# A four-part layer stack on one core: the even layer's output projection in three rounded passes, six probability buffers instead of four, and the next ffn's first weights split after the fifth output tile

## The chip, the cores and the metric

The kernel runs on one core of one Trainium2 chip. The metric is the device time of one launch in microseconds (us), taken over several runs; beside it stands one profiled execution of the same program, from which all rows below come. TensorE is called PE in the rows, VectorE DVE, ScalarE ACT, GpSimd POOL and SyncE SP.

## The reference, cut to what matters

Two layers over 256 latent tokens and 256 context tokens of width 1024, float32 throughout. Each layer is half an ffn, a mixer, half an ffn, each with a residual and a layer norm:

```python
x = half_ffn(x, mod_l, 0, ffn_a, ...);  cx = half_ffn(cx, mod_c, 0, ffn_a, ...)
hl, hc = modulate(x, mod_l, 1), modulate(cx, mod_c, 1)
yc, yl = even_mixer(hc @ ev_w_in, hl @ ev_w_in, ...)      # layer 0; layer 1 has odd_mixer
x = layer_norm(alpha * x + gate(mod_l, 1) * (yl @ w_out), ln_g, ln_b)
x = half_ffn(x, mod_l, 2, ffn_b, ...)
# the same for cx in layer 0
```

The even mixer has two halves of 512 columns each. The first is attention with 8 heads of 64: context queries see the 256 context keys, latent queries see all 512 keys with a bias, and each row gets a softmax. The second is a two-way mLSTM with 4 heads of 128, whose output is centred and scaled per head. `yc` and `yl` are both halves side by side; `w_out` is 1024 x 1024.

## The kernel before

All activations lie feature-major: `h`, `m` and `y` (which is `m` under another name) are 8 tiles of 128 features by 512 tokens, context in columns 0 to 255, latent in 256 to 511. The stages follow each other: ffn0, even, ffn1, ffn2, odd, ffn3. Each engine's program is written out by hand in its own block, and semaphores order them; there is no planner. So what runs when is set by the order of the code in a block and by the `wait_ge` calls.

**Products in parts.** Nearly all products with the input and ffn weights are made in three passes: weights and inputs are each split into a rounded part (type fp32r, `w_hi`, `m_hi`), which ACT makes as a copy, and the rest (`w_lo`, `m_lo`), which DVE makes as a subtraction, in place. Then PE adds hi x hi, hi x lo and lo x hi. The output projection of the mixers (`out_proj`, lines 790, 800 and 807) does not do this: it multiplies float32 by float32 directly, and each such product of 128x512 shows in the trace as two MATMUL instructions (64 of L790 in the even stage for 32 calls).

**The attention stage** goes over 16 pairs of units (a unit is one head, one stream, one tile of 128 queries). In a round of four pairs, two are of context queries (256 keys) and two of latent queries (512 keys). For a pair p, PE makes the scores (L950), DVE the negated row maxima (`maxima`: L2480, or L2482 to L2484 with the bias, written to `probs`), ACT the exponentials (L1627), DVE the reciprocal and the scaling (L2492, L2495), PE four or eight transposes (L979), ACT copies them (L1638), PE weighs the values (`weigh`, L962) once in two pairs, and DVE copies the result to `y` (`attention_out`, L2580). On DVE `maxima(p + 1)` stands ahead of the scaling of pair p, and it begins with

```python
if p >= 2:
    dve.wait_ge(sem("na_pT_done"), 2 * p - 2)
```

because `probs` has four buffers: unit u writes buffer `u % 4`, which the transposes of the pair two earlier must have read.

**The mLSTM stage** follows, eight steps v of: DVE exponents (L2513), ACT exponentials (L1669, L1671), DVE products (L2556), PE (L1026), DVE quotients (L2522 and on). Behind each second one the head is centred, and ACT takes its squares (L1679).

**The output projection.** In the first half four output tiles d = 0 to 3 grow side by side, one input tile c after another. Between c = 2 and c = 3 PE transposes the mLSTM heads (`turn_heads`, L1035), and for d = 2 of c = 0 it waits until the last mLSTM banks are read. Tiles d = 4, 5 and 6 follow one by one, and tile 7 is made for the context stream and then the latent stream, with the sums for the layer norm (`norm_stats`, L772, L773, L778, L780) of the context inside the latter. DVE adds each tile to `h` (L2019, tile 7 L2040), ACT squares it (L1360), POOL keeps the running sums of both (L2716 and L2722). Behind tile 6 DVE makes the first two `w_lo` of the next ffn (`first_weights`, L1979) and folds the modulation (`fold`); ACT makes the `w_hi` (L1277) at the same place. `first_tile` of the ffn (L700, L701, L696) then begins with the first normalised tile. The odd stage ends in the same way, for the latent stream alone, with float32 products too.

## Time and profile before

| | |
|---|---|
| median of 3 runs | 1960.8 us (1959.03 to 1961.54) |
| the profiled execution's own time | 1961.69 us |
| its span, first to last instruction | 1960.0 us |
| mean granted TensorE clock | 0.967 of full speed |
| PE busy | 95% of the span |
| DVE, ACT, POOL busy | 69%, 35%, 15% |

A timeline row gives the start in us from the span's start, the duration in us, engine, line, operation, output<-input with shapes, and how many instructions were merged; in brackets stands the idle time of the engine ahead of it and what ended that. The end of a MATMUL is modelled, so the distance between starts says more than durations. The granted clock is given as a share of 2.4 GHz; its two levels are 1.2 and 2.4 GHz.

### The profile page before, as it was taken

The page shows a single profiled execution, that of the slowest core. Times are in us where ns is not written, and L with a number is a line of the kernel's source. Part 1 is how long each engine was busy: PE and PEld are TensorE (multiplying, and loading weights), DVE is VectorE, ACT ScalarE, POOL GpSimd, SP SyncE. Part 2 cuts the span into 40 slices and gives each one's busy share as a digit, 9 for nine tenths or more (in the row PEclk, how much of TensorE's full clock was granted, in tenths as well). Part 3 has the DMA queues.
Part 4 walks back from the last instruction along what each step waited for, and adds up shares of the span by engine and source line. Part 5 has one row for each costly group of instructions (what it writes and reads, how often), then busy time and mean ns, then how long its engine had stood idle before and what let it go on. Part 6 is the DMA issues. An engine that isn't in the chain of part 4 may idle for free. (4 is left out here: it accounts for less than half of the span.)

```text
span 1960.0 us, 25249 instructions
## 1 busy us (share of the span) xinstructions
PE 1862.0 (95%) x9616; PEld 1559.0 (80%) x9616; DVE 1354.9 (69%) x2331; ACT 692.2 (35%) x1143; POOL 301.9 (15%) x313
## 2 busy tenths in 40 slices
PE   6999999999997789899999999999999999989997
PEld 6888878898784455788887888888878898879997
DVE  7677777869975563877778357774687887564454
ACT  3222233345444431422224233222242543434443
POOL 0000001143000003400000232000044445140002
PEclk7999999999897899899999999999999999989999
DMA  9355444215431101454544233554234545405533
GB/s 360 129 195 204 171 188 166 98 56 138 151 147 59 44 1 43 165 201 171 207 152 174 102 123 122 211 193 153 107 111 169 214 175 204 170 3 186 198 150 111
DMA packets 43963, 290.17 MB, mean 148 GB/s; under 512 B 13916, under 2 KB 19676, under 8 KB 27232
## 3 DMA queue, kind: packets, MB, share of 16 engines
q1 hardware_dynamic: 35488, 271.13, 37.7%
q10 hardware_dynamic: 8384, 17.83, 2.4%
q8 instruction: 58, 0.95, 0.2%
q14 instruction: 33, 0.27, 0.0%
HBM read 272.16 MB, written 16.78 MB: 147 GB/s over the span
## 5 line engine op out<-in xcount | busy, mean ns | idle before, releaser
L1930 DVE CUSTOM_DVE_ANT_0 L<-slot 128x1024 f32<-128x1024 f32 x272 | 339.5, 1248 | 82.3 <-DMA slot<-in_ada_dram 75.1
L1277 ACT ACTIVATE w_hi<-slot 128x1024 fp32r<-128x1024 f32 x176 | 186.3, 1061 | 573.5 <-PE bank L681 558.2
L1979 DVE TENSOR_TENSOR w_lo<-slot,w_hi 128x1024 fp32r<-128x1024 f32 x176 | 216.8, 1234 | 204.4 <-ACT w_hi L1277 197.9
L676 PE MATMUL bank<-m_hi,w_hi 128*128 128x512 f32 (+1 forms) x1344 | 296.6, 363 | 3.2 <-ACT w_hi L1277 3.2
L681 PE MATMUL bank<-m_hi,w_lo 128*128 128x512 f32 (+1 forms) x1344 | 296.2, 363 | 0.1
L678 PE MATMUL bank<-m_lo,w_hi 128*128 128x512 f32 (+1 forms) x1344 | 296.1, 363 | 0.0
L676 PEld LDWEIGHTS bank<-m_hi,w_hi 128*128 128x128 f32 x1344 | 232.3, 189 | 43.1 <-ACT w_hi L1277 4.0
L681 PEld LDWEIGHTS bank<-m_hi,w_lo 128*128 128x128 f32 x1344 | 232.5, 189 | 39.7 <-DVE w_lo L1979 0.5
L678 PEld LDWEIGHTS bank<-m_lo,w_hi 128*128 128x128 f32 x1344 | 232.6, 189 | 39.3
L2160 DVE TENSOR_TENSOR down_lo<-slot,down_hi 128x1408 fp32r<-128x1408 f32 x64 | 108.8, 1716 | 116.1 <-ACT down_hi L1326 115.8
L739 PE MATMUL bank<-g_lo,down_hi 128*128 128x512 f32 (+1 forms) x770 | 154.7, 349 | 0.1
L739 PEld LDWEIGHTS bank<-g_lo,down_hi 128*128 128x128 f32 x770 | 126.7, 190 | 19.0 <-DVE g_lo L2166 0.6
L2714 POOL COPY L<-h 128x512 f32<-128x512 f32 (+1 forms) x6 | 3.7, 613 | 883.0 <-DVE h L2019 883.0
L1326 ACT ACTIVATE down_hi<-slot 128x1408 fp32r<-128x1408 f32 x64 | 87.5, 1377 | 146.6 <-PE bank L742 111.4
L733 PE MATMUL bank<-g_hi_mid,down_hi 128*128 128x512 f32 (+1 forms) x420 | 97.9, 361 | 1.9 <-ACT g_hi_mid L1336 1.6
L742 PE MATMUL bank<-g_hi_mid,down_lo 128*128 128x512 f32 (+1 forms) x420 | 88.7, 347 | 0.0
L733 PEld LDWEIGHTS bank<-g_hi_mid,down_hi 128*128 128x128 f32 x420 | 70.8, 191 | 19.9 <-ACT g_hi_mid L1336 10.1
L742 PEld LDWEIGHTS bank<-g_hi_mid,down_lo 128*128 128x128 f32 x420 | 69.5, 189 | 9.9
L2716 POOL TENSOR_TENSOR L<-L,h 128x512 f32<-128x512 f32 (+1 forms) x36 | 44.1, 1224 | 215.4 <-DVE h L2019 214.9
L1360 ACT ACTIVATE L<-h 128x512 f32<-128x512 f32 (+1 forms) x42 | 23.5, 560 | 139.6 <-DVE h L2019 134.9
L2733 POOL TENSOR_TENSOR h<-h,L 128x256 f32<-128x256 f32 x79 | 64.7, 851 | 38.7 <-DVE L L2048 38.7
L2019 DVE SCALAR_TENSOR_TENSOR h<-bank,mgate,h 128x256 f32<-128x256 f32 x70 | 30.8, 477 | 40.8 <-PE bank L800 26.9
(393 smaller groups left out, 2929.8 us busy)
## 6 DMA issues: line engine op xcount, KB each, us to landing
slot<-in_gateup_dram SPq DMA_DIRECT2D x44, 2048.0 KB, 8.1
slot<-in_ada_dram SPq DMA_DIRECT2D x34, 2048.0 KB, 8.1
slot<-in_down_dram SPq DMA_DIRECT2D x32, 1408.0 KB, 6.4
slot<-in_ev_in_dram SPq DMA_DIRECT2D x4, 2048.0 KB, 8.8
slot<-in_od_in_dram SPq DMA_DIRECT2D x4, 2048.0 KB, 9.5
R<-s_ops SPq DMA_DIRECT2D x16, 512.0 KB, 5.7
s_tables<-slot ACTq DMA_DIRECT2D x8, 768.0 KB, 3.3
R<-s_tables SPq DMA_DIRECT2D x8, 768.0 KB, 6.7
```

Of the source, the lines that this page charges most:

```text
L676: nc.tensor.matmul(bank[j][:, c0:T], w_hi[:, off, c, :], m_hi[:, c, c0:T], start=(c == 0), stop=False)
L678: nc.tensor.matmul(bank[j][:, c0:T], w_hi[:, off, c, :], m_lo[:, c, c0:T], start=False, stop=False)
L681: last = nc.tensor.matmul(bank[j][:, c0:T], w_lo[b][:, 2 * j + off, c, :], m_hi[:, c, c0:T], start=False, stop=(c == KT - 1))
L733: nc.tensor.matmul(out_d, down_hi[:, half, f % HALF, :], g_hi(f)[:, a:b], start=(f == 0), stop=False)
L739: nc.tensor.matmul(out_d, down_hi[:, half, f % HALF, :], g_lo[:, f, a:b], start=False, stop=False)
L742: last = nc.tensor.matmul(out_d, down_lo[k - 3][:, half, f % HALF, :], g_hi(f)[:, a:b], start=False, stop=(f == FT - 1))
L1277: nc.scalar.activation(w_hi[:, off, :, :].rearrange("p a b -> p (a b)"), slots[b][:, (2 * (f % 2) + off) * D:(2 * (f % 2) + off + 1) * D], ...
L1326: nc.scalar.activation(down_hi[:, half, :, :].rearrange("p a b -> p (a b)"), slots[k][:, half * HALF * P:(half + 1) * HALF * P], ACT.Copy) ...
L1930: ins = nc.vector.tensor_tensor_reduce(out=junk, in0=slots[k][:, t * D:(t + 1) * D], in1=csilu[s_], scale=1.0, scalar=0.0, op0=ALU.mult, o ...
L1979: nc.vector.tensor_tensor(w_lo[b][:, t, :, :].rearrange("p a b -> p (a b)"), slots[b][:, t * D:(t + 1) * D], w_hi[:, off, :, :].bitcast(F3 ...
L2160: nc.vector.tensor_tensor(down_lo[d % 2][:, half, :, :].rearrange("p a b -> p (a b)"), slots[3 + d % 2][:, half * HALF * P:(half + 1) * HA ...
L2733: nc.gpsimd.tensor_tensor(h[:, d, a:b], h[:, d, a:b], mean[:, a:b], ALU.subtract).then_inc(sem("c"), 1)
```

## The change

Three edits. (1) The even output projection becomes `even_out_proj`: inputs and weights are split like everywhere else, and PE makes three passes of fp32r products. ACT gets 8 rounded copies of `y` tiles and 8 of weight parts, DVE as many subtractions. Where they stand: `y` tiles 0 to 3 ahead of the mLSTM (ACT) and behind its first exponents (DVE); weight parts 0 to 2 on ACT behind the exponentials of v = 1, part 3 behind those of v = 6, parts 4 to 7 behind the squares of head 2; on DVE part 0 in v = 1, part 1 in v = 3, parts 2 and 3 in v = 7; `y` 4 to 7 and parts 4 to 7 behind the last `y` tile. (2) `probs` has six buffers, and `maxima(p)` waits for the transposes of the pair three earlier. (3) In the even and the odd stage `first_weights` and `fold` move from behind tile 6 to behind tile 4 on DVE, and on ACT from behind all squares to behind the fifth.

```diff
-        probs = [L[:, 0:T], L[:, T:2 * T], R[:, 12288:12288 + T], R[:, 5120:5120 + T]]
+        probs = [L[:, 0:T], L[:, T:2 * T], R[:, 12288:12288 + T], R[:, 5120:5120 + T], L[:, 6 * T:7 * T], L[:, 7 * T:8 * T]]
...
+            def even_out_proj(between):
...
+                def inputs_rest(c):
+
+                    lo("y", c)
+                    for d in range(4):
+                        last = nc.tensor.matmul(proj_out(name, d)[:, :], out_hi[d][:, c, :], m_lo[:, c, :], start=False, stop=(c == KT - 1))
+                        if c == KT - 1:
+                            last.then_inc(used[0] if d == 3 else sem("even_out_done"), 1)
+
+                take(0)
+                for c in range(KT):
+                    hi("y", c)
+                    for d in range(4):
+                        if c == 0 and d == 2:
+                            pe.wait_ge(sem("ml_out_read"), 2 * HEADS)
+                        if c == 0:
+                            hi("w", d)
+                            lo("w", d)
+                        nc.tensor.matmul(proj_out(name, d)[:, :], out_hi[d][:, c, :], even_y_hi[:, c, :], start=(c == 0), stop=False)
+                        nc.tensor.matmul(proj_out(name, d)[:, :], w_lo[0][:, d, c, :], even_y_hi[:, c, :], start=False, stop=False)
+                    if c:
+                        inputs_rest(c - 1)
+                    if c == 2:
+                        between()
+                inputs_rest(KT - 1)
+                take(1)
+                for d in range(4, KT - 1):
+                    pe.wait_ge(sem("r_ready"), before("r_ready", name) + d - 3)
+                    hi("w", d)
+                    for c in range(KT):
+                        nc.tensor.matmul(proj_out(name, d)[:, :], out_hi[d][:, c, :], even_y_hi[:, c, :], start=(c == 0), stop=False)
+                    for c in range(KT):
+                        nc.tensor.matmul(proj_out(name, d)[:, :], out_hi[d][:, c, :], m_lo[:, c, :], start=False, stop=False)
+                    lo("w", d)
+                    for c in range(KT):
+                        last = nc.tensor.matmul(proj_out(name, d)[:, :], w_lo[1][:, d % 4, c, :], even_y_hi[:, c, :], start=False, stop=(c == KT - 1))
...
+                    if name in ("even", "odd") and d == 4:
+                        for off in range(2):
+                            weights_hi(1 if name == "even" else 3, 0, off)
...
-                if name in ("even", "odd"):
-                    first_weights()
...
+                        if st == 0 and u >= 6:
+                            act.wait_ge(sem("na_pT_done"), u - 5)
...
+                    if hd == 0:
+                        act.wait_ge(full[0], 16 * (uses_before("ffn1")[0]))
+                        for d in range(3):
+                            out_weights_hi(d)
...
+                act.wait_ge(full[1], 16 * (uses_before("ffn1")[1]))
+                act.wait_ge(sem("ml_scores_done"), HEADS)
+                act.wait_ge(sem("ml_out_done"), 2 * HEADS - 1)
+                for d in range(4, KT):
+                    out_weights_hi(d)
...
-                first_weights(n)
-                fold(n + 1)
+                    if d == 4:
+                        first_weights(n)
+                        fold(n + 1)
...
-                    if p >= 2:
-                        dve.wait_ge(sem("na_pT_done"), 2 * p - 2)
+                    if p >= 3:
+                        dve.wait_ge(sem("na_pT_done"), 2 * p - 4)
...
+                        for d in {1: (0,), 3: (1,), 7: (2, 3)}.get(v, ()):
+                            out_weights_lo(d)
```

The order of PE's instructions from the last mLSTM product on, before the change (`m` holds `y`, `slot` the weights, L1035 the transposes of the heads; a row counts calls, each of which the float32 product turns into two instructions in the trace):

```order
L1026 MATMUL bank<-R 128x129 x20
L790 MATMUL bank<-m,slot 128x512 x12
L1035 MATMUL bank<-ident,R 128x128 x16
L790 MATMUL bank<-m,slot 128x512 x20
L800 MATMUL bank<-m,slot 128x512 x24
L807 MATMUL bank<-m,slot 128x256 x12
```

and the same place after it, for the end of the first half (the last four `inputs_rest` of c = 6 and c = 7 stand together) and the next tile:

```order
L839 MATMUL bank<-even_y_hi,out_hi 128x512
L840 MATMUL bank<-even_y_hi,w_lo 128x512
L826 MATMUL bank<-m_lo,out_hi 128x512 x8
L851 MATMUL bank<-even_y_hi,out_hi 128x512 x8
L853 MATMUL bank<-m_lo,out_hi 128x512 x8
L856 MATMUL bank<-even_y_hi,w_lo 128x512 x8
```

What was 8 calls for a tile is now 24, of a cheaper kind. DVE behind the last `y` tile, before (L2570 writes `y`, L1991 the gate, L2019 are the residuals of tiles 0 to 6, two each, then come the first weights and `fold`, and L2040 is tile 7):

```order
L2570 SCALAR_TENSOR_TENSOR m<-bank,ml_gn,R 128x512 x4
L1991 TENSOR_SCALAR mgate<-mods 128x16
L2019 SCALAR_TENSOR_TENSOR h<-bank,mgate,h 128x256 x14
L1979 TENSOR_TENSOR w_lo<-slot,w_hi 128x1024 x2
L2002 TENSOR_SCALAR mscale<-mods 128x16
```

and after (the same instructions have lines 2673, 2078, 2106, 2066 and 2089; L2127 is tile 7):

```order
L2673 SCALAR_TENSOR_TENSOR m<-bank,ml_gn,R 128x512 x4
L2639 TENSOR_TENSOR m_lo<-m,even_y_hi 128x512 x4
L2644 TENSOR_TENSOR w_lo<-slot,out_hi 128x1024 x4
L2078 TENSOR_SCALAR mgate<-mods 128x16
L2106 SCALAR_TENSOR_TENSOR h<-bank,mgate,h 128x256 x10
L2066 TENSOR_TENSOR w_lo<-slot,w_hi 128x1024 x2
L2089 TENSOR_SCALAR mscale<-mods 128x16
L2091 TENSOR_TENSOR mshift<-mscale,lnb 128x16
L2092 TENSOR_TENSOR mshift<-mshift,mods 128x16
L2093 TENSOR_TENSOR mscale<-mscale,lng 128x16
L2106 SCALAR_TENSOR_TENSOR h<-bank,mgate,h 128x256 x4
L2127 SCALAR_TENSOR_TENSOR h<-bank,mgate,h 128x256
```

Eight subtractions are new ahead of the first residual, and the first weights now stand ahead of the residuals of tiles 5 and 6. ACT in the mLSTM stage, from the exponentials of v = 1 to those of v = 2 (L1744 is what was L1671, L1742 what was L1669):

```order
L1744 ACTIVATE R<-bank,acol 128x128
L1719 ACTIVATE out_hi<-slot 128x1024 x3
L1742 ACTIVATE R<-R 128x4x128
L1744 ACTIVATE R<-bank,acol 128x384
L1744 ACTIVATE R<-bank,acol 128x256
```

The three copies L1719 are new there; the others kept their order.

## Rows read from the trace of the kernel before

**Rows 1.** The page: busy time of the engines.

```profile
PE 1862.0 (95%) x9616; PEld 1559.0 (80%) x9616; DVE 1354.9 (69%) x2331; ACT 692.2 (35%) x1143; POOL 301.9 (15%) x313
```

**Rows 2.** Timeline, even stage: three-pass tiles (L874 to L879), then 256-column products.

```profile
449.97 1.98 PE L874 MATMUL bank<-even_m_hi,part_hi 128*128 128x512 f32 x8
...
455.41 1.98 PE L874 MATMUL bank<-even_m_hi,part_hi 128*128 128x512 f32 x8
...
440.23 0.28 PE L851 MATMUL bank<-even_m_hi,first_hi 128*128 128x256 f32 x1
440.35 0.28 PE L852 MATMUL bank<-even_m_hi,w_lo 128*128 128x256 f32 x1
```

**Rows 3.** Timeline, the first half of the even output projection.

```profile
723.43 1.88 PE L790 MATMUL bank<-m,slot 128*128 128x512 f32 x4
...
725.55 8.85 PE L790 MATMUL bank<-m,slot 128*128 128x512 f32 x20 [0.24 <-DVE R L2533]
...
731.06 2.49 DVE L2567 TENSOR_TENSOR R<-R 128x512 f32<-128x512 f32 x4
...
750.84 3.39 DVE L2019 SCALAR_TENSOR_TENSOR h<-bank,mgate,h 128x256 f32<-128x256 f32 x8 [13.15 <-issue]
```

**Rows 4.** Timeline, from tile 4 to the first product of ffn1.

```profile
753.15 20.76 PE L800 MATMUL bank<-m,slot 128*128 128x512 f32 x48
...
773.75 5.34 PE L807 MATMUL bank<-m,slot 128*128 128x256 f32 x24
...
776.47 3.23 DVE L1979 TENSOR_TENSOR w_lo<-slot,w_hi 128x1024 fp32r<-128x1024 f32 x2 [1.64 <-ACT w_hi L1277]
...
780.73 0.70 PE L778 MATMUL bank<-h,mean_w 128*128 128x256 f32 x2 [0.77 <-DVE h L2040]
...
788.69 0.55 PE L700 MATMUL bank<-m_hi,w_hi 128*128 128x256 f32 x1 [1.59 <-ACT m_hi L1251]
```

**Rows 5.** The page: ACT and DVE weight parts, POOL's sums (mean ns last before the bar).

```profile
L1277 ACT ACTIVATE w_hi<-slot 128x1024 fp32r<-128x1024 f32 x176 | 186.3, 1061 | 573.5 <-PE bank L681 558.2
L1979 DVE TENSOR_TENSOR w_lo<-slot,w_hi 128x1024 fp32r<-128x1024 f32 x176 | 216.8, 1234 | 204.4 <-ACT w_hi L1277 197.9
...
L2716 POOL TENSOR_TENSOR L<-L,h 128x512 f32<-128x512 f32 (+1 forms) x36 | 44.1, 1224 | 215.4 <-DVE h L2019 214.9
```

**Rows 6.** Timeline, mLSTM stage: where ACT and DVE wait.

```profile
679.42 0.63 ACT L1669 ACTIVATE R<-R 128x512 f32<-128x512 f32 x1 [4.11 <-DVE R L2513]
...
681.51 0.23 DVE L2522 SCALAR_TENSOR_TENSOR R<-bank,R 128x2 f32<-128x2 f32 x2 [2.13 <-PE bank L1026]
...
723.63 0.23 DVE L2522 SCALAR_TENSOR_TENSOR R<-bank,R 128x2 f32<-128x2 f32 x2 [3.34 <-PE bank L1026]
```

**Rows 7.** Two rounds of attention by windows: us, busy and instructions by engine, clock, DMA.

```profile
610.41:626.29 15.88, 12.24 (x66) 6.63 (x68) 11.13 (x30) 8.67 (x24) 0.00 (x0) 0.82 0.00 0
626.29:641.17 14.88, 11.24 (x66) 6.25 (x68) 11.04 (x30) 8.67 (x24) 0.00 (x0) 0.84 0.00 0
```

**Rows 8.** Who DVE waited for, 593 to 662.8: total us, times, longest.

```profile
DVE col L2480 <- PE bank L979: 9.9, 6, 1.9
...
DVE L L2482 <- PE bank L979: 3.6, 4, 2.0
DVE R L2482 <- PE bank L979: 2.8, 4, 2.2
```

**Rows 9.** Timeline, the first round of attention.

```profile
600.66 0.47 ACT L1627 ACTIVATE R<-bank,col 128x256 f32<-128x256 f32 x1 [4.41 <-DMA s_local<-R]
...
604.89 0.42 DVE L2482 COPY R<-bank 128x256 f32<-128x256 f32 x1 [2.17 <-PE bank L979]
```

**Rows 10.** Timeline, the end of the odd stage.

```profile
1734.69 3.62 PE L807 MATMUL bank<-m,slot 128*128 128x256 f32 x16
...
1740.20 0.70 PE L778 MATMUL bank<-h,mean_w 128*128 128x256 f32 x2 [1.03 <-DVE h L2040]
```

**Rows 11.** Windows: PE's last mLSTM products (columns as in rows 7).

```profile
719.40:723.40 4.00, 4.00 (x20) 3.88 (x21) 0.89 (x4) 0.00 (x0) 0.00 (x0) 0.57 0.00 0
```

More of the change, by code:

```diff
@@ L793, in out_proj @@
                             last.then_inc(used[slot_pair[0]] if d == 3 else sem(f"{name}_out_done"), 1)
-                    if c == 2 and between:
-                        between()
                 take(slot_pair[1])
@@ L808, in out_proj @@
                                                 start=(c == 0), stop=(c == KT - 1))
-                        if c == 3 and s_ == 1 and name == "even":
+                    last.then_inc(used[slot_pair[1]] if s_ == 1 else sem("ctx_out_done"), 1)
+                norm_stats(name, 1)
+            def even_out_proj(between):
+                name = "even"
+                hi = lambda what, n: pe.wait_ge(sem("part_hi_ready"), EVEN_OUT_AT + OUT_HI.index((what, n)) + 1)
+                lo = lambda what, n: pe.wait_ge(sem("part_lo_ready"), EVEN_OUT_AT + OUT_LO.index((what, n)) + 1)
+                def inputs_rest(c):
[31 more added lines that the diff above has]
+                        last = nc.tensor.matmul(proj_out(name, d)[:, :], w_lo[1][:, d % 4, c, :], even_y_hi[:, c, :], start=False, stop=(c == KT - 1))
+                    last.then_inc(sem("even_out_done"), 1)
+                pe.wait_ge(sem("r_ready"), before("r_ready", name) + KT - 4)
+                hi("w", KT - 1)
+                lo("w", KT - 1)
+                for s_ in range(2):
+                    a, b = STREAMS[s_]
+                    for c in range(KT):
+                        nc.tensor.matmul(last_out(name, s_)[:, a:b], out_hi[KT - 1][:, c, :], even_y_hi[:, c, a:b], start=(c == 0), stop=False)
+                    for c in range(KT):
+                        nc.tensor.matmul(last_out(name, s_)[:, a:b], out_hi[KT - 1][:, c, :], m_lo[:, c, a:b], start=False, stop=False)
+                        last = nc.tensor.matmul(last_out(name, s_)[:, a:b], w_lo[1][:, 3, c, :], even_y_hi[:, c, a:b], start=False, stop=(c == KT - 1))
+                        if c == 3 and s_ == 1:
@@ L1036, in turn_heads @@
                         last.then_inc(sem("ml_turned"), 1)
-                out_proj("even", (0, 1), 0, turn_heads)
+                even_out_proj(turn_heads)
             def head_means(name, c0):
@@ L1648, in even, with out_inputs_hi, out_weights_hi @@
                     turned_probs(p)
+                def out_inputs_hi(c):
+                    act.wait_ge(*((sem("even_y0"), 2 * (c + 1)) if c < 4 else (sem("even_y1"), c - 3)))
+                    nc.scalar.activation(even_y_hi[:, c, :], y[:, c, :], ACT.Copy).then_inc(sem("part_hi_ready"), 1)
+                def out_weights_hi(d):
+                    nc.scalar.activation(out_hi[d][:, :, :].rearrange("p a b -> p (a b)"), slots[d // 4][:, (d % 4) * D:(d % 4 + 1) * D], ACT.Copy).then_inc(sem("part_hi_ready"), 1)
+                act.wait_ge(sem("na_probs_ready"), 2 * NA_PAIRS)
+                for c in range(4):
+                    out_inputs_hi(c)
                 slot_done[3] += 1
@@ L1692, in even @@
                 nc.scalar.activation(ml_var, ml_var, ACT.Sqrt).then_inc(sem("ml_var_ready"), 1)
+                for c in range(4, KT):
+                    out_inputs_hi(c)
                 squares("even", 0)
@@ L2571, in even @@
                                                    ALU.mult, ALU.mult).then_inc(sem("even_y1"), 1)
+                for c in range(4, KT):
+                    out_inputs_lo(c)
+                for d in range(4, KT):
+                    out_weights_lo(d)
                 out_residual(1, "even", (0, 1), 0)
```

51 lines of the change are left out of this document (34 added, 17 removed).

## The prediction

> **What bounds the kernel now.** I read the page first: PE is busy 95% of the span, DVE 69% [rows 1]. So a stage gets shorter either by fewer PE cycles or by taking away what PE waits for, and most stages offer little. Then I read three stretches in the timeline, those that the change touches: attention (593 to 663 us), the even projection with the norm behind it (723 to 789), and the end of the odd stage. The reader should see in each which engine the others wait for.
>
> In the even projection it is PE alone: 48 instructions of tiles 4 to 6 follow each other from 753.15 to 773.75, 6.87 us for a tile, while DVE had stood idle 13.15 us before the first residual [rows 3, 4]. In attention it is no single engine: in a round of four pairs PE, DVE and ACT are busy 12.2, 11.1 and 8.7 of 15.9 us [rows 7], and DVE waits for the transposes L979 16.3 us in all (9.9 + 3.6 + 2.8) [rows 8]. That is a chain: transposes of pair p - 1, maxima of p + 1, scaling of p, transposes of p.
>
> **Edit 1, three passes: the price of a product.** Tiles with the same operand types and shape run in the even stage already: 24 instructions take 455.41 - 449.97 = 5.44 us, 0.227 us each, at full clock [rows 2]. The tile costs 6.87 us now. So a tile of 512 columns gets 1.43 us cheaper. With 256 columns the distance is 0.12 us [rows 2], so a stream of tile 7 takes 24 x 0.12 = 2.9 us against 16 x 0.215 = 3.4 now (half of 0.429, which is 6.87 over 16). The Trainium skill ("TensorE: Matmul & The Clock Gate", Back-to-back issue gap) gives N / 2.4 GHz + 2.5 ns, 216 ns for 512 columns. By it a tile would take 5.18 us and the eight tiles another 2 us less, an estimate; the trace shows 227 ns where the weights change with each product, and I go by the trace.
>
> First half, walked through. PE starts at 723.43 and does four products (0.9 us), to 724.3. Then it waits for the bank that DVE frees, until 725.55 [rows 3]: a float32 pair of tiles filled that time until now, with 0.24 us left. The 28 products up to the head transposes take 6.35 us, to 731.9. The heads become ready from 731.06 on, the last at 733.55 (2.49 us for four [rows 3]); the transposes behind it end about 734.1. The other 64 products take 14.5 us, to 748.6. The last product of tile 0 is over 0.7 us earlier; its residual follows 0.26 us later and takes 0.85 (3.39 us for eight of L2019, two for a tile [rows 3]), and tile 4 needs its bank: start at 749.2 instead of 753.15 [rows 4]. **3.9 us.**
>
> Second half. Three tiles at 5.44 end at 765.5 instead of 773.75. The context stream takes 2.9 us, the latent stream has 16 instead of 8 products ahead of the norm's sums (1.9 us), and these need two float32 products of two instructions each, 0.9 us, before L778. That puts L778 at 771.3. Before it stood at 780.73, 0.77 us of this being the wait for DVE's L2040, which stood behind the first weights (3.23 us from 776.47) and `fold` [rows 4]. In the new order the context residual can be made at 768.7, when PE has it. **The stretch to L778 gains 9.4 us**, the 3.9 included. From L778 to the first product of ffn1, 788.69, a chain of DVE, ACT and POOL takes 7.96 us [rows 4]; nothing in it changes, so 9.4 us arrive at ffn1, which is bound by PE.
>
> **What hides the new work.** ACT: a weight copy costs 1.06 us [rows 5]. Three stand behind v = 1, where ACT has 4.11 us idle before 679.42 [rows 6]: 3.2 fit, 0.9 are left. Parts 3 to 7 lie in later idle stretches; without cover each would cost 1.06. Behind a late copy there stand the next exponentials, and PE and DVE wait for those. DVE: a weight rest costs 1.23 us [rows 5]. One stands in v = 1 where DVE waits 2.13 us, one in the like place of v = 3, two in v = 7 where it waits 3.34 for 2.5 [rows 6]. The four `y` rests and four weight rests behind the last `y` tile cost 4 x 0.65 + 4 x 1.23 = 7.5 us (0.65 from L2567, 2.49 us for four [rows 3]). The 13.15 us idle there [rows 3] shrink by about 3 us, since PE is earlier, and take it. The first residual queues behind them; I reckon about 743.5 for their end against 748.2 when it is due. So all of it is costed at nothing; from the other side, if each gap were short by a third, 2 to 3 us.
>
> The first weights behind tile 4 need the next ffn's slot 0, whose load is issued when the first half ends. If that is late, ACT's sixth square and DVE's sixth residual queue behind it. PE waits for neither, since tile 7 needs only the residual of tile 3; POOL does, with 1.22 us an addition [rows 5], two for a tile. By my walk it is through with tile 6 at 769.2, where the sums are wanted at 770.4. Slack is 1.2 us, so this edit costs nothing or, at worst, 1 us.
>
> **Edit 2, six buffers.** With the wait moved back by one pair, DVE no longer waits for L979. How much of the 16.3 us comes back elsewhere the trace doesn't show, so I bound it. From above: a round cannot be shorter than DVE's 11.1 busy us, and in the first round ACT is held by a DMA until 600.66 [rows 9] whatever DVE does; 16.3 less some 2 gives 14 us. From below nothing is excluded but a loss, as no wait is added that isn't met: say 3.5. In between I walk one round. `attention_out` behind a latent pair has only 0.8 + 0.2 + 0.9 us of DVE work ahead of it (two short maxima, reciprocal, scaling), where PE needs the eight transposes and the weighing, 3.3 to 4: a wait of 1.3 to 2. Another 0.5 us falls where maxima want scores that stand behind the weighing. So a round takes 11.1 + 1.8 to 2.5, about 13.3, against a mean of 15.4 [rows 7]: 2.1 us for each of two full rounds. In the first round the maxima at 604.89 [rows 9] move up to when their scores are there, about 602.9: 2.0. In the last round the tail of transposes, copies and weighing stays, and I take 1. **7 us**, nearer the lower bound than the upper since two engines besides DVE are busy over half the time.
>
> **Edit 3 in the odd stage.** PE ends tile 7 at 1738.3, makes the first two sums until 1739.2 and waits 1.03 us for L2040, to 1740.20 [rows 10]; this wait goes. The ffn3 weights have long been loaded. **1.0 us.**
>
> **Sum.** 9.4 + 7 + 1.0 = 17.4 us. The profiled execution took 1961.69 us, 1.7 more than its span, so it would take 1944.3. It lies 0.9 us over the median of 1960.8; from the median I get 1943.4, and forecast 1943.5.
>
> **The rivals.** Within 0.2% is 4 us, about what a measurement of this kernel can tell from no change.
>
> - *The forecast*, 1940 to 1947, chance 0.67.
> - *The attention waits come back*: PE, with weighing and scores in order and a clock of 0.82 [rows 7], or ACT takes DVE's place, and only 3 to 4 us are gained. 1947 to 1950, chance 0.13. For it speaks PE's 12.2 us in a round, against it that PE too waits for DVE before most transposes.
> - *Attention reaches DVE's bound*: 1936 to 1939.5, chance 0.07. A denser PE could also get a higher clock there.
> - *The side work shows*, or PE's 1.2 us wait at 724.3 brings the lower clock for some us. Just before it PE runs at 0.57 after a wait [rows 11], then at full clock in the projection. 2 to 5 us: 1945.5 to 1949, chance 0.07.
> - *Slower*, chance 0.03: the clock. PE needs 43.8 us for the new projection at 2.4 GHz (21.8 + 16.3 + 5.8). At 1.2 GHz all through it would need twice that and the kernel would take 1987; the sign turns when 17.4 of the 43.8 us are run at the lower level. The densest PE work has full clock in the trace, so it is unlikely. A second way to the same side are weight loads that are not hidden: 0.162 us each (1559.0 us for 9616 [rows 1]) on 24 products is 3.9 us a tile instead of nothing, which turns the gain of 1.43 into a loss of 2.4 and ends at 1974. Rows 2 show 24 loads inside 5.44 us, so I give it 0.01 of the 0.03. The Trainium skill ("TensorE: Matmul & The Clock Gate", What overlaps and what doesn't) has the rule behind it: a load overlaps with running products only where the row group differs, which full 128-row products never do. The trace does not agree.
> - *No change that can be told*: several of the gains fail together, chance 0.03.
>
> **How the numbers follow.** The likeliest case gives 1943.5. From 1938 to 1950 it takes in the forecast, the second and fourth case and part of the third, some 0.88 of the chance on paper; I keep that width because the size of edit 2 is bounded so loosely. Faster 0.94, same 0.03, slower 0.03.
>
> **What the changed profile would show.** Right: tile 4 of the projection starts 25.8 us after its first product instead of 29.7; tiles 4 to 6 are 5.4 us apart; no idle time of PE before the context L778; from the first product of the projection to the first of ffn1 55.8 us instead of 65.3; DVE waits for the transposes of L979 near zero, and instead for L962; rounds of 13 to 13.5 us; ACT's exponentials of v = 2 start no later behind those of v = 1. Wrong: rounds above 14.5 us, a DVE wait for ACT's weight copies, POOL ending its sums after PE wants them, or a granted clock below 1 between the first product and the norm.

## The result, and the profile after

The changed kernel takes 1939.43 us, median of 4 runs (1937.61 to 1942.06), the kernel before beside it 1960.72 (1959.03 to 1961.54). The ratio is 0.9889, 95% interval 0.9873 to 0.9906: 21 us faster, 4 us more than the 17.4 of my sum, and inside the range of 1938 to 1950. The profiled execution took 1940.38 us with a span of 1938.7, against 1961.69 and 1960.0.

The page of after, first part (beside [rows 1]):

```profile
PE 1848.0 (95%) x9688; PEld 1567.4 (81%) x9688; DVE 1368.4 (71%) x2347; ACT 704.7 (36%) x1159; POOL 302.5 (16%) x313
```

PE has 14 us less to do, although it has 72 instructions more; DVE and ACT got 13.5 and 12.5 us more, the parts of the projection's operands.

Timeline of after, the even projection (beside [rows 3] and [rows 4]): first product, the wait for the bank, the heads, the end of the first half, tiles 4 to 7, the context sums, ffn1.

```profile
717.21 0.47 PE L839 MATMUL bank<-even_y_hi,out_hi 128*128 128x512 f32 x1
...
719.40 0.50 PE L839 MATMUL bank<-even_y_hi,out_hi 128*128 128x512 f32 x1 [1.03 <-DVE R L2621]
...
725.89 2.17 PE L1094 MATMUL bank<-ident,R 128*128 128x128 f32 x16
...
742.02 3.23 DVE L2106 SCALAR_TENSOR_TENSOR h<-bank,mgate,h 128x256 f32<-128x256 f32 x8 [5.01 <-issue]
...
748.57 1.98 PE L851 MATMUL bank<-even_y_hi,out_hi 128*128 128x512 f32 x8
...
754.01 1.98 PE L851 MATMUL bank<-even_y_hi,out_hi 128*128 128x512 f32 x8
...
759.45 1.12 PE L864 MATMUL bank<-even_y_hi,out_hi 128*128 128x256 f32 x8
...
762.32 1.12 PE L864 MATMUL bank<-even_y_hi,out_hi 128*128 128x256 f32 x8
...
765.10 0.59 PE L784 MATMUL bank<-h,mean_w 128*128 128x256 f32 x2
...
772.95 0.55 PE L706 MATMUL bank<-m_hi,w_hi 128*128 128x256 f32 x1 [1.58 <-ACT m_hi L1310]
```

Tiles start 5.57 and then 5.44 us apart, a stream of tile 7 takes 2.87, the sums of L784 follow without idle time, and from the first product to ffn1 it is 55.74 us instead of 65.26. Tile 4 starts at 743.00, 25.79 us behind the first product.

Who DVE waited for in attention, after (592.5 to 655.5), beside [rows 8]:

```profile
DVE col L2568 <- PE bank L1009: 9.8, 4, 8.1
DVE m L2687 <- PE bank L1021: 8.7, 5, 4.0
DVE L L2570 <- PE bank L1009: 4.3, 4, 1.4
DVE R L2570 <- PE bank L1009: 1.2, 1, 1.2
```

The transposes (L1038 now, L979 before) are gone from the list; DVE waits for scores (L1009) and for the weighed group (L1021). The longest wait, 8.1 us, lies ahead of the stage's first maxima, as it did before.

**Stage by stage.** The same landmarks in several profiles, each stretch from one first instruction to the next (us; differences of starts in the timelines, the last column from the span rounded to 0.1 us). Between scan part and odd end lie 50.8 us that are alike in all of them:

```
                         attention  mLSTM  projection  ffn1,ffn2  odd: scan  odd: end  ffn3 to
                                           and norm    and on     part       and norm  the end
before                     68.96    60.50    65.26      788.52     106.69     12.28    213.03
before_again               68.91    60.50    65.26      788.61     106.73     12.29    212.87
after                      62.98    61.74    55.74      789.39     103.68     10.99    210.90
after_again                64.34    59.83    55.87      788.75     103.52     10.98    210.51
e1_attention               64.27    58.45    65.25      788.33     103.82     12.28    212.63
e2_projection              68.55    60.45    57.23      788.74     103.81     12.29    211.59
e3_first_parts             68.91    60.50    64.21      788.79     107.61     10.99    213.42
e4_late_first_parts        62.29    60.37    57.18      788.71     104.03     12.29    212.24
e5_scores_first            61.84    60.43    55.78      790.17     103.65     10.99    210.57
e6_bank_wait_filled        61.67    60.36    55.76      789.45     103.70     10.98    210.80
e7_act_waits               68.83    60.49    65.27      788.58     103.76     12.29    212.84
e8_pe_waits                70.95    59.98    65.30      788.85     103.65     12.29    211.33
e9_wait_kept               68.80    60.41    55.76      789.44     103.64     10.98    210.44
e10_scale_first            59.73    62.60    55.72      788.36     103.66     10.98    211.11
```

The two profiles of the comparison differ by 21.3 us: 1.5 ahead of attention (before_again reaches it at 591.53, before at 593.97, so this differs between executions of one program), 6.0 in attention, -1.2 in mLSTM, 9.5 in projection and norm, -0.9 in the ffns, 3.0 in the scan part, 1.3 at the odd end, 2.1 in ffn3. The stretches from attention to norm and the odd end give 15.6 (17.4 forecast, 1.8 less); scan part and ffn3, which no edit touches, give 5.1. That is what the experiments had to explain.

### The profile page after: what moved, and what is told of

The parts are those of the page before. It is cut to its first block and busy times, and to the rows that moved or that the text cites. A ratio compares the mean times of both kernels' runs of the same rounds, so it can differ in the third digit from the quotient of the medians.

```text
span 1938.7 us, 25445 instructions
## 1 busy us (share of the span) xinstructions
PE 1848.0 (95%) x9688; PEld 1567.4 (81%) x9688; DVE 1368.4 (71%) x2347; ACT 704.7 (36%) x1159; POOL 302.5 (16%) x313
## 5 line engine op out<-in xcount | busy, mean ns | idle before, releaser
L745 PEld LDWEIGHTS bank<-g_lo,down_hi 128*128 128x128 f32 x770 | 126.6, 190 | 19.1 <-DVE g_lo L2253 0.9
L706 PE MATMUL bank<-m_hi,w_hi 128*128 128x256 f32 x112 | 38.5, 358 | 19.7 <-ACT m_hi L1310 14.4
```

The source lines that it names most:

```text
L745: nc.tensor.matmul(out_d, down_hi[:, half, f % HALF, :], g_lo[:, f, a:b], start=False, stop=False)
```

## The experiments

Measured times are medians of 4 to 12 executions (before_again has one). In brackets stand the ratio to the kernel before on the same chip and its 95% interval. The ratio isn't always that of the two medians, and a gain "by the ratio" is reckoned from it. In the expectations, theory A and theory B are the two answers that the run should tell apart. They count the mLSTM stage between other landmarks than the table (56.5 us there are 60.5 here).

**Each edit alone, and the change without edit 3.** e1_attention is the kernel before with edit 2. These are its two main places; the buffers' indices and the `col` tile change with them, and ACT gets twelve waits:

```diff
-probs = [L[:, 0:T], L[:, T:2 * T], R[:, 12288:12288 + T], R[:, 5120:5120 + T]]
+probs = [L[:, 0:T], L[:, T:2 * T], R[:, 12288:12288 + T], R[:, 5120:5120 + T], L[:, 6 * T:7 * T], L[:, 7 * T:8 * T]]
-                    if p >= 2:
-                        dve.wait_ge(sem("na_pT_done"), 2 * p - 2)
+                    if p >= 3:
+                        dve.wait_ge(sem("na_pT_done"), 2 * p - 4)
```

> Only edit 2 (six probability buffers). Theory A, each edit gives in its own stretch what the profiles of before and after show there: attention gets 6.0 us shorter (68.96 to 62.98 us between the first scores and the first mLSTM product), the mLSTM stage keeps its 56.5 us since no projection work lies in it, and the kernel gains 6 us: 1954 to 1955.5. Theory B, the buffers also set something later in motion, so that the gain of some 4 us that my sum doesn't explain (odd stage and ffn3) comes with them: 1950 to 1952.

Measured 1951.22 us (0.9946, 0.9933 to 0.9960). e2_projection is the kernel before with `even_out_proj` and the parts it needs:

```diff
-                out_proj("even", (0, 1), 0, turn_heads)
+                even_out_proj(turn_heads)
```

> Only edit 1 (even projection in three passes). Theory A: 30 us of float32 tiles become 25.8 up to tile 4, tile 5 and 6 and the last tile follow as after the whole change, but the first weights of ffn1 still lie behind tile 6 on DVE, so PE's wait before the context sums comes back (0.8 us or more); mLSTM pays 1.4 us for the weight copies in it. Net 7 to 8 us: 1952.5 to 1954. Theory B, the unexplained 4 us belong to this edit: 1948 to 1950. Rival on the mLSTM stage: if its 1.4 us were only a matter of clock episodes and not of the added copies, this kernel's mLSTM stage lasts 56.5 us and not 57.8.

Measured 1948.21 us (0.9930, 0.9916 to 0.9943). e3_first_parts:

```diff
                     residual(n, name, d, proj_out(name, d), c0)
-                first_weights(n)
-                fold(n + 1)
+                    if d == 4:
+                        first_weights(n)
+                        fold(n + 1)
```

with the same move on ACT.

> Only edit 3 (the next ffn's first parts beside the fifth output tile, in the even and the odd stage). Theory A: PE's waits before the norm's sums go, 0.77 us in the even stage and 1.03 in the odd one: 1.8 to 2 us, 1958.8. Theory B, it also gives the 4 us in odd stage and ffn3: 1954 to 1956. Rival: DVE and GpSimd in each other's way behind tile 4 make the residuals late and give back some of it: 1960 to 1961.

Measured 1956.11 us (0.9973, 0.9963 to 0.9983). e4_late_first_parts is the whole change with this last diff undone.

> The whole change without edit 3 (the first parts stand behind tile 6 again, in both stages). Theory A: with the faster projection PE overtakes DVE more than before, since the tiles' residuals come every 5.44 us and the parts still take 3.2 us: the wait before the context sums is 0.8 to 2 us, the odd stage has its 1.03 us wait again, so this kernel is 2 to 3 us slower than the whole change: 1941.5 to 1942.5. Theory B, edit 3 is worth nothing by itself: within 0.5 us of the whole change.

Measured 1943.14 us (0.9904, 0.9889 to 0.9919), 3 to 4 us slower than the whole change (2.7 by the stretches of the table). The timeline of e4_late_first_parts shows the wait that comes back, and what DVE does at the time:

```profile
765.67 0.70 PE L784 MATMUL bank<-h,mean_w 128*128 128x256 f32 x2 [1.21 <-DVE h L2126]
...
761.37 3.26 DVE L2065 TENSOR_TENSOR w_lo<-slot,w_hi 128x1024 fp32r<-128x1024 f32 x2 [1.65 <-ACT w_hi L1336]
...
765.14 0.47 DVE L2126 SCALAR_TENSOR_TENSOR h<-bank,mgate,h 128x256 f32<-128x256 f32 x1
```

In its own stretch each edit gives about what theory A says: attention 4.7 us (6.0 expected), projection and norm 8.0, edit 3 1.05 in the even and 1.3 in the odd stage. Beside the faster projection edit 3 is worth 1.3 to 1.4 in the even stage, since PE overtakes DVE by more.

The weight copies cost nothing in the mLSTM stage. It lasts 60.45 us with them (e2_projection) and 60.50 without, but 58.45 in e1_attention, which has no copies either, and 61.74 in the first profile of after. Windows of the stage, before, e1_attention and after:

```profile
662.93:723.43 60.50, 51.46 (x224) 34.17 (x225) 38.99 (x140) 23.52 (x68) 0.00 (x0) 0.92 0.10 35
657.55:716.00 58.45, 49.40 (x224) 32.47 (x225) 38.99 (x140) 23.52 (x68) 0.00 (x0) 0.94 0.10 37
655.47:717.21 61.74, 52.70 (x225) 35.20 (x225) 45.85 (x148) 31.71 (x77) 0.00 (x0) 0.89 0.09 35
```

Stretch minus busy time is PE's idle time: 9.04, 9.05 and 9.04 us, and 9.0 to 9.1 in all 14 profiles. Only the busy time of the same products differs, and with it goes the granted clock, 0.94 to 0.88. So neither the copies nor any other edit makes PE wait more in this stage.

But the medians of the three kernels lie where theory B put them, or nearer to it than to theory A. Each edit alone gained more than its stretch: 10.6, 13.7 and 5.3 us by the ratios, 29.6 in all, where the three together give 22. The difference is less certain than it looks: each gain has an interval of 2 to 2.8 us to either side, and all three are measured against the same 13 executions of the kernel before, whose median of 1961.47 is the highest on record (1959.3 to 1960.8 in the other sets). In the profiles 2.9 us of the surplus of e1 and of e2 lie in the scan part of the odd stage, and 2.05 of e1's in mLSTM, by the clock. For e3 the profile doesn't show it: that execution took 1959.90 us, the longest of nine (from 1953.21).

**The same kernels again.**

> The changed kernel once more, for a second profile. Theory A, of the 21.3 us between the two profiles some 4 have no edit in their stretch (odd stage's scan part 3.0, ffn3's end 1.8, start of attention 1.5, against it mLSTM's loss): those that are luck of the clock or of a transfer differ again between this profile and the first. Theory B, they belong to the program: every stretch repeats within 0.3 us.

> The kernel before once more, for a second profile. Theory A, its odd stage shows a GpSimd wait of 1.8 us with half clock behind it only in some executions, so that this profile lasts 2 to 3 us less there. Theory B, the wait and the half clock are there again (scan part 106.7 us), and the changed kernels' 103.8 is something they gain by being earlier or later against the loads.

Measured 1939.50 us (0.9884, 0.9864 to 0.9903) and 1959.18 (one run). Theory A fell for the scan part: 106.73 us again in the kernel before, 103.52 in the changed one. It held for attention (64.34 against 62.98) and mLSTM (59.83 against 61.74), and the stretch ahead of attention (593.71 against 592.49).

**A change of nothing but instruction streams.** e7_act_waits is the kernel before with

```diff
                         src = score_banks[u % 4][:, 0:keys] if st == 0 else probs[u % 4][:, :]
+                        if st == 0 and u >= 6:
+                            act.wait_ge(sem("na_pT_done"), u - 5)
```

> The kernel before, with nothing but the twelve extra waits that the six buffers bring to ScalarE's instruction stream, each already fulfilled; no buffer, no operation and no order is changed. Scan part of the odd stage (first L1087 to first L1183): 106.7 us in both profiles of before and 107.6 with edit 3 alone, 103.7 to 103.9 in the six others, whatever edit they hold. Theory A, where the instruction fetches fall decides whether that stage's table lands late (an instruction fetch of ScalarE's and the small engines' queue stands 0.6 us before the landing in all three slow profiles and in none of the others): it takes 103.8 us here, kernel 1957 to 1958.5. Theory B, the 3 us come with an edit's own work or with being some 8 us earlier: 106.7 us, kernel as before, 1960.5. Attention 68.9 us by both.

and e8_pe_waits the kernel before with 302 such calls in front of the transposes, which make 151 instructions of PE (`EXTRA[u]` is 20 or 18 for even u, else 0):

```diff
+                        for _ in range(EXTRA[u]):
+                            pe.wait_ge(sem("even_acol_ready"), 2)
                         pe.wait_ge(sem("na_probs_ready"), u + 1)
```

> The kernel before, with 151 more instructions in PE's stream that only wait for what is long fulfilled, spread over attention where PE idles: as many as the three-pass projection adds. From the first product of ffn3 to the end: 212.9 to 213.4 us in the profiles without edit 1, 210.5 to 212.2 with it, by waits for copies of down weights whose transfers land late. Theory A, the shift of PE's instruction fetches decides it: 211 to 212 us here, and the kernel 1 to 2 us faster unless the waits cost as much in attention (bounds 0 to 3 us). Theory B, it doesn't: 213 us, the kernel as before or slower by what attention shows. Scan part of the odd stage stays at 106.7 us by both.

Both took the 3 us out of the scan part in their profiles, and e8 1.5 to 1.7 out of ffn3 too. First the kernel before, then e7_act_waits, both in the timeline, PE at the end of the scan part:

```profile
1666.88 2.21 PE L1117 MATMUL bank<-slot,R 128*128 128x64 f32 x16 [1.77 <-POOL slot L2800]
```

```profile
1663.44 1.97 PE L1117 MATMUL bank<-slot,R 128*128 128x64 f32 x16 [0.53 <-POOL slot L2802]
```

And windows of the two, ten us from the start of that product (columns as in [rows 7]):

```profile
1666.88:1676.88 10.00, 10.00 (x50) 7.24 (x51) 5.70 (x8) 7.36 (x17) 4.38 (x4) 0.83 0.01 2
```

```profile
1663.44:1673.44 10.00, 10.00 (x64) 8.09 (x65) 6.77 (x10) 8.80 (x18) 4.29 (x4) 1.00 0.01 2
```

The wait is 1.2 us shorter, and behind it PE's granted clock stays at 1.00, where behind the long wait it falls to a mean of 0.83: 1.2 us come of the wait and 1.7 of what follows it. The wait begins with a table (`s_tables`) whose transfer lands late: 10.7 us after its issue at 1634.24 in the kernel before, 9.5 in e7_act_waits, 8.2 in e8_pe_waits. The DMA answers from 2.2 us ahead of that issue on to the landing, before, e7_act_waits and e8_pe_waits:

```profile
q14 instruction: 1, 0.01, 0.6%
q8 instruction: 1, 0.02, 0.4%
slot<-in_od_in_dram SPq DMA_DIRECT2D x1, 2048.0 KB, 10.5
```

```profile
q8 instruction: 1, 0.02, 0.7%
slot<-in_od_in_dram SPq DMA_DIRECT2D x1, 2048.0 KB, 9.3
```

```profile
q14 instruction: 1, 0.01, 0.8%
slot<-in_od_in_dram SPq DMA_DIRECT2D x1, 2048.0 KB, 8.6
```

A transfer of instructions starts between the issue and the landing of this table in none of the 14 profiles. What differs is how many stand just ahead of it, beside the start of the 2048 KB weight load: one of queue 8, 2.0 to 2.5 us ahead of the table's issue, and one of queue 14, 1.1 to 1.6 us ahead. With both, in before, before_again and e3_first_parts, the table took 10.2 to 11.2 us to land; with that of queue 8 alone, in e7_act_waits and e1_attention, 9.5 and 9.2; with that of queue 14 alone, in e8_pe_waits, 8.2; with none, in the eight others, 8.3 to 8.9. So the recorded expectation of e7_act_waits has the time of the transfer wrong (0.6 us before the landing), and e8_pe_waits still has the transfer of queue 14 that theory A blamed, without a late landing. That the two transfers together hold the table up goes with all 14 profiles, but is argued and not shown.

In the executions that weren't profiled the effect can't be told from nothing. e7_act_waits took 1959.25 us; it gains 2.2 us by its ratio (0.9989, 0.9978 to 1.0000) and 0.4 by the two medians, and neither theory's kernel time (1957 to 1958.5, 1960.5) was met. e8_pe_waits gains nothing (0.9997, 0.9985 to 1.0009; 1959.36 us), having lost 2.0 us in attention by its own waits. So two kernels with nothing but fulfilled waits added have a scan part that is 3 us shorter in their profiles; how often the late landing meets an execution that isn't profiled is not known. That e8 changes the scan part too was expected by neither theory.

**What edit 2 consists of, and what bounds a round now.** e9_wait_kept is the changed kernel with

```diff
-                    if p >= 3:
-                        dve.wait_ge(sem("na_pT_done"), 2 * p - 4)
+                    if p >= 2:
+                        dve.wait_ge(sem("na_pT_done"), 2 * p - 2)
```

> The changed kernel with six buffers, but the wait of the maxima for the transposes left where it stood before (pair p - 2 instead of p - 3). Theory A, the gain of attention (4.6 to 7.3 us) is this wait alone: attention back at 68.5 to 69.5 us, DVE waiting some 16 us for the transposes again, kernel 1945 to 1946.5. Theory B, a part comes from elsewhere (another place in memory for two of the buffers, ScalarE's exponentials): attention 65 to 67 us.

Measured 1945.05 us (0.9920, 0.9906 to 0.9935). Who DVE waited for in its attention:

```profile
DVE col L2568 <- PE bank L1038: 9.6, 6, 1.8
...
DVE L L2570 <- PE bank L1038: 5.8, 6, 2.2
DVE R L2570 <- PE bank L1038: 0.7, 2, 0.5
```

16.1 us for the transposes, as the 16.3 of [rows 8], and 68.80 us for the stage. Theory A holds: the gain is this wait, 5 to 7 us.

What it is made of shows in windows of the whole stage, before, e9_wait_kept, after and after_again:

```profile
593.97:662.93 68.96, 49.82 (x258) 26.82 (x257) 44.52 (x120) 34.97 (x98) 0.85 (x3) 0.78 0.09 39
593.72:662.52 68.80, 49.72 (x259) 26.69 (x257) 44.55 (x120) 36.66 (x102) 0.85 (x3) 0.78 0.09 39
592.49:655.47 62.98, 47.70 (x258) 25.93 (x257) 44.22 (x120) 36.16 (x102) 0.85 (x3) 0.81 0.10 42
593.71:658.05 64.34, 49.33 (x259) 26.20 (x257) 44.26 (x120) 36.14 (x102) 0.85 (x3) 0.79 0.10 41
```

PE stands idle 19.1 us with the old wait and 14.9 to 15.3 with the new one, in all five profiles that have this attention (these two, e1_attention, e4_late_first_parts and e6_bank_wait_filled): 3.9 to 4.2 us are waits that went. The rest of the gain, 0.5 to 3.2 us, is PE's busy time, 49.8 us before and 49.4 to 46.6 after, and goes with the granted clock, 0.79 to 0.83 instead of 0.78.

e5_scores_first is the changed kernel with PE's scores of p + 3 ahead of `weigh`, and DVE's copy behind the next maxima:

```diff
                     if p and p % 2 == 0:
+                        if p + 3 < NA_PAIRS:
+                            scores(p + 3)
                         weigh(p // 2 - 1)
```

> The changed kernel, with attention's order turned at one place of each round: PE makes the scores of pair p + 3 ahead of weighing the finished group (p even), and DVE copies the weighed group after the next maxima instead of before them. Theory A, what is left of a round (14.0 us against the 13.3 of my prediction) is DVE standing behind PE's weighing and the scores queued after it, 2.7 and 1.6 us in the two full rounds (1.96 + 0.76, 0.85 + the scores' wait): the rounds fall to 12 to 12.8 us, attention to 57 to 60 us from 63.0, and the kernel gains 3 to 5 us over the changed one: 1934.5 to 1936.5. Theory B, a round is bound by the chain through DVE's scaling and PE's transposes (PE waits 10.2 us for the scaling in all): rounds stay within 0.3 us of 14.0 and the kernel at 1939.5.

Measured 1938.60 us (0.9879, 0.9861 to 0.9898); rounds 13.77 and 13.79, attention 61.84. That is in the middle between the theories until it is held against e6_bank_wait_filled, whose attention is that of the changed kernel and took 61.67, rounds 13.65 and 13.73. So the new order gave nothing, and the rounds stay within 0.3 us of 14.0: theory A fell.

e10_scale_first has, beside the filled bank wait, one more turn of DVE's order:

```diff
-                    if p + 1 < NA_PAIRS:
+                    if p + 1 < NA_PAIRS and p % 4 != 2:
                         maxima(p + 1)
...
+                    if p % 4 == 2:
+                        maxima(p + 1)
```

the second one behind the scaling of pair p.

> The changed kernel with the filled bank wait of e6_bank_wait_filled, and in each group of attention DVE scales the first latent pair ahead of the maxima of the second one. Theory A, the round (13.65 and 13.73 us in that kernel) is set by the chain through DVE's scaling and PE's transposes: the exponentials of this pair are done 2.6 us before DVE takes them up, and PE waits 2.62 us for them, once in a round; the scaling moves up, PE's wait goes, and of the 2.6 us 1.1 are paid back since the next exponentials start later. Rounds of 11.8 to 12.8 us, attention 57 to 60 us from 61.7, kernel 1934 to 1937 against 1938.3. Theory B, DVE's and ScalarE's own work (11.0 and 8.6 us busy in a round) and the order of the maxima bound the round: it stays at 13.5 to 14 us, or gets longer by 1 us, and the kernel at 1938 to 1942.

Measured 1938.19 us (0.9889, 0.9868 to 0.9910). Two rounds of e6_bank_wait_filled by windows, then two of e10_scale_first:

```profile
618.94:632.59 13.65, 11.03 (x64) 6.28 (x64) 10.95 (x31) 8.57 (x25) 0.00 (x0) 0.88 0.00 0
632.59:646.32 13.73, 10.45 (x60) 5.98 (x61) 11.03 (x31) 8.57 (x25) 0.00 (x0) 0.87 0.01 2
```

```profile
619.27:632.30 13.03, 11.21 (x64) 6.20 (x64) 10.85 (x30) 8.55 (x25) 0.00 (x0) 0.87 0.00 1
632.30:645.56 13.26, 10.82 (x60) 5.77 (x60) 10.27 (x28) 8.48 (x25) 0.00 (x0) 0.87 0.00 1
```

The chain through the scaling is part of the bound: a round loses 0.5 to 0.6 us, not the 0.9 to 1.9 of theory A, and attention 1.9. That is one profile, but its rounds are shorter than those of every other. All of it was lost again behind it, and the kernel's median lies in theory B's 1938 to 1942. Attention and mLSTM by windows, e6_bank_wait_filled, then e10_scale_first:

```profile
592.48:654.15 61.67, 46.60 (x259) 26.14 (x257) 44.26 (x120) 36.29 (x102) 0.85 (x3) 0.83 0.11 43
654.15:714.51 60.36, 51.31 (x224) 34.13 (x225) 45.98 (x148) 31.77 (x77) 0.00 (x0) 0.92 0.10 36
```

```profile
593.05:652.78 59.73, 47.65 (x259) 25.11 (x257) 43.96 (x120) 35.76 (x102) 0.85 (x3) 0.81 0.11 45
652.78:715.38 62.60, 53.56 (x224) 32.99 (x225) 45.76 (x148) 31.71 (x77) 0.00 (x0) 0.88 0.09 34
```

In attention PE's idle time fell from 15.1 to 12.1 us, while its busy time grew by 1.05 at a clock of 0.81 instead of 0.83. With the same mLSTM instructions the granted clock is 0.88 instead of 0.92, PE is busy 2.2 us longer, and the stage is 2.2 us longer. Whether the denser attention brings this about or it is chance, one profile doesn't tell: with the new wait the stage took 58.45 to 62.60 us in seven profiles, with the old one 59.98 to 60.50 in seven.

**Is the projection bound by PE alone?** e6_bank_wait_filled is the changed kernel with

```diff
+                for c in range(2):
+                    with_inputs_hi(c, (0, 1))
+                pe.wait_ge(sem("ml_out_read"), 2 * HEADS)
                 for c in range(KT):
+                    with_inputs_hi(c, (2, 3) if c < 2 else range(4))
```

where `with_inputs_hi(c, tiles)` makes the products of `y` tile c with the two weight parts of these output tiles.

> The changed kernel, with PE's only wait inside the projection filled: the products of the second y tile for output tiles 0 and 1 come before the wait for the banks of tiles 2 and 3. Theory A, the whole projection is bound by PE's products: the wait of 1.03 us goes and tile 4 starts about 1.0 us earlier behind the first product (24.8 us instead of 25.8), kernel 1 us faster, 1938.5. Theory B, the chain of the four heads (DVE's z, PE's transposes, y and its parts) has no slack: the first transposes start no earlier, and nothing or less than 0.3 us is gained.

Measured 1938.31 us (0.9879, 0.9860 to 0.9898). Its timeline has no wait for a bank, and this one instead:

```profile
722.92 2.46 PE L1099 MATMUL bank<-ident,R 128*128 128x128 f32 x16 [0.47 <-DVE R L2675]
```

Tile 4 starts 25.81 us after the first product (25.79 without the edit), and from the first product to ffn1 it is 55.76 us. PE reaches the heads' transposes 0.3 us sooner and stands in front of DVE's z; from there on both kernels run alike. Theory B: the chain of the heads has no slack, and the first half's 25.8 us are its length as much as PE's work. The median is the one that theory A named, but the projection has no part in it; the two kernels' intervals overlap.

## Why the prediction was right, point by point

- *The price of a product.* 5.43 to 5.44 us for a tile of 512 columns, 2.87 for a stream of tile 7: as read from [rows 2]. Of the weight loads: the 56 us of projection and norm hold 41.6 us of loads beside 50.7 of products, so most of them are hidden. The Trainium skill ("TensorE: Matmul & The Clock Gate", What overlaps and what doesn't) says that a weight load overlaps with running products only where the row group differs; these loads all take the full 128 rows, and the trace does not agree: 92.3 us of both fit in 55.7.
- *First half.* 3.9 us forecast; tile 4 came 25.79 us after the first product for 25.8. The number is right. My walk took it from PE's work, and e6_bank_wait_filled shows that the heads' chain bounds it too.
- *To the context sums and ffn1.* 9.4 us forecast, 9.5 measured; PE's idle time is gone.
- *What hides the new work.* The weight copies cost nothing (PE's idle time in mLSTM is 9.0 us with and without them), and ACT's exponentials of v = 2 start 5.99 us behind those of v = 1, as before (5.98). The rests and parts on DVE were through at 737.0; reckoned were 743.5 on the clock of the kernel before, 737.3 here, since the projection starts 6.2 us earlier. DVE then stood idle 5.0 us until the first residual was due, at 742.02. Behind tile 4 it was tighter than I had it: DVE's weight rests and POOL's sums lie side by side, and both get longer. Timeline of after:

```profile
752.03 3.46 DVE L2066 TENSOR_TENSOR w_lo<-slot,w_hi 128x1024 fp32r<-128x1024 f32 x2 [2.39 <-ACT w_hi L1336]
755.41 1.25 DVE L2089 TENSOR_SCALAR mscale<-mods 128x16 f32<-128x16 f32 x1
...
752.20 2.21 POOL L2823 TENSOR_TENSOR L<-L,h 128x512 f32<-128x512 f32 x1
754.37 2.27 POOL L2829 TENSOR_TENSOR L<-L 128x512 f32<-128x512 f32 x1
...
761.98 1.29 POOL L2829 TENSOR_TENSOR L<-L 128x512 f32<-128x512 f32 x1
```

  The row of the two DVE subtractions hides what happens: the first takes 1.22 us, its usual time, and the second 2.32. The POOL addition that starts 0.17 us behind the first one takes 2.21 us instead of 1.29, and the next, begun beside the second one, 2.27. The first `fold` instruction takes 1.25 us instead of the 0.16 of e4_late_first_parts, and ends 0.04 us behind that addition. So the two engines take turns, and whichever starts second ends about its own time after the other. The sums end at 763.27, PE wants them at 764.24: 1.0 us of slack are left, 1.2 were forecast. (The slot's load landed 0.6 us after ACT wanted it, another thing that the prediction had as a risk.) The Trainium skill ("SBUF — State Buffer", Who interferes with whom) says that a VectorE instruction with two SBUF inputs and a GpSimd one that reads SBUF contend for a shared port pair; for the subtractions and additions the trace agrees. The `fold` instruction has one SBUF input, so that sentence doesn't account for it.
- *Attention.* 7 us forecast, 6.0, 4.6, 4.7, 6.7 and 7.3 measured (after, after_again, e1_attention, e4_late_first_parts, e6_bank_wait_filled). The mechanism is right (e9_wait_kept), but the term was sized by waits alone, and these gave 3.9 to 4.2 us; what came on top is a higher clock, which the sum did not have and which differs from one execution to the next. The rounds are 13.65 to 14.0 us for 13.3: in the two full rounds I had counted 1.8 to 2.5 us of DVE waits, and it is 2.7 to 3.
- *Odd stage.* 1.0 us forecast, 1.3 measured; the residual is no longer in the way. Timeline of after, without the 1.03 us of [rows 10]:

```profile
1721.13 0.59 PE L784 MATMUL bank<-h,mean_w 128*128 128x256 f32 x2
```

- *The step that was missing* is the term for stages without an edit, which I set to nothing. The edits' stretches gave 15.6 of 17.4 us, attention 1.0 and mLSTM 1.2 less than forecast and the others 0.4 more; scan part and ffn3 gave 5.1, and the start and the other ffns 0.6. In the scan part a PE wait that is 1.2 us shorter and the higher clock behind it make up the 3 us; why the table lands earlier is argued, not shown.
- *What is luck in the number.* The sum is only 4 us off because two misses have opposite signs. The median of 1939.43 lies just outside the case that I gave 0.67 (1940 to 1947) and in the band of "attention reaches DVE's bound" (1936 to 1939.5), which did not happen: the rounds are 13.65 to 14.0 us, DVE's work in them 11. Without the 5.1 us the kernel would be at about 1944.5, in the range too.
- *Rivals.* Neither a lower clock in the projection (0.99 in projection and norm, in both kernels) nor the attention waits coming back in full was seen.

Still open: why e3_first_parts gains 5.3 us in the medians with 2.3 in its two stretches; what share of the 2.0 to 2.5 us in ffn3 goes with the streams (e8_pe_waits took 1.5 to 1.7 of them); and what sets the granted clock in attention and mLSTM apart from one execution to the next.

## What to carry to other kernels

A wait that frees a buffer should be costed by what the waiting engine meets next: here 16 us of waits were worth 5 to 7, since PE's scores and weighing were next in line. Split such a gain into the bound engine's idle time and its busy time: the first repeated within 0.4 us, the second came and went with the clock. Before filling a wait of the bound engine, look for the chain that meets it a few instructions on. And an edit that adds instructions can move a stage that it doesn't touch by some us: test the edits one by one, and if their gains don't add up, test a kernel that holds only fulfilled waits, before believing in any part of a few us.

## What the runs showed of the hardware that I had not expected

- Twelve fulfilled waits on ScalarE, and nothing else, made a stage that starts some 900 us later 2.9 us shorter (106.69 to 103.76 us, one profile with them and two without; the medians don't show it). The table's landing went from 10.7 to 9.5 us.
- Of two DVE subtractions of 128x1024 beside POOL's additions one took 1.22 us and the other 2.32, against 1.24 on the page's mean; the additions of 128x512 2.21 and 2.27 us against 1.29. An instruction over 16 columns took 1.25 instead of 0.16 us there and ended with the addition, within 0.05 us, in the six profiles of kernels that hold edits 1 and 3; in the eight others it took 0.16.
- With one program, attention took 62.98 and 64.34 us, at a mean granted clock of 0.81 and 0.79. With the old wait it was 68.80 to 68.96 us at 0.78 in before, before_again, e3_first_parts, e7_act_waits and e9_wait_kept, and 68.55 at 0.80 in e2_projection.
- In the mLSTM stage PE stood idle 9.0 to 9.1 us in all 14 profiles, while the stage took 58.45 to 62.60 us.
